# A two-block kernel on one core: unit matrix and scaled receptances of the WKV step matrices added by VectorE on eviction

## What is computed

```python
def step(s, inp):
    r_t, lw_t, k_t, v_t, a_t, b_t = inp
    sa = jnp.einsum('dbhij,dbhj->dbhi', s, a_t)
    s = s * jnp.exp(lw_t)[..., None, :] + sa[..., None] * b_t[..., None, :] + v_t[..., None] * k_t[..., None, :]
    return s, jnp.einsum('dbhij,dbhj->dbhi', s, r_t)

def rwkv_run(prep, s0):
    r, logw, k_dir, v, a_vec, b, gate = prep
    return wkv_scan(orient_shared(r), orient_dir(logw), orient_dir(k_dir), orient_shared(v),
                    orient_shared(a_vec), orient_dir(b), s0)
...
bonus = jnp.sum(r[None] * k_dir * r_k, axis=(0, -1))[..., None] * v
o = (yn + bonus.reshape(B, T, D)) * jax.nn.silu(gate)
```

## Time and profile before

| | |
|---|---|
| runs | 2570.5, 2577.51, 2576.24 us; median 2576.24 |
| profiled execution | 2568.52 us |
| its span | 2566.8 us |
| granted TensorE clock, mean | 0.937 |
| TensorE busy | 2276.0 us (89%), 16920 records |
| DVE busy | 974.0 us (38%) |
| ACT busy | 522.6 us (20%) |
| POOL busy | 319.0 us (12%) |

### The profile page before, as it was taken

The page is one execution under the profiler, slowest core; times in us unless marked ns, Lnnn a source line. Parts: engine busy times, 40 slices in busy tenths (PEclk is TensorE's granted clock), DMA queues, the critical chain, the costliest instruction groups (busy, mean ns, idle before and its releaser), DMA issues. The chain is left out here.

```text
span 2566.8 us, 40218 instructions
## 1 busy us (share of the span) xinstructions
PE 2276.0 (89%) x16920; PEld 1682.1 (66%) x16920; DVE 974.0 (38%) x2194; ACT 522.6 (20%) x926; POOL 319.0 (12%) x558
## 2 busy tenths in 40 slices
PE   2999966789999999999998688999998899879998
PEld 1888855578788886688873345565566667446546
DVE  3124436430343057277316244424424531120253
ACT  1011012320100010200013334333333422011142
POOL 0000000000000030000003544333432011000000
PEclk9999987799999999999999789998999889889989
DMA  7455520414686421187504665545544241313100
GB/s 298 184 225 218 197 100 0 81 23 161 273 303 232 177 104 50 66 332 297 207 1 163 215 171 161 148 124 139 137 122 110 49 112 44 150 51 117 47 1 17
DMA packets 126267, 359.75 MB, mean 140 GB/s; under 512 B 78600, under 2 KB 87048, under 8 KB 108304
## 3 DMA queue, kind: packets, MB, share of 16 engines
q1 hardware_dynamic: 93776, 213.05, 24.2%
q0 software_dynamic: 31744, 143.16, 16.5%
q10 hardware_dynamic: 576, 1.05, 0.1%
HBM read 340.36 MB, written 16.85 MB: 139 GB/s over the span
## 5 line engine op out<-in xcount | busy, mean ns | idle before, releaser
L271 PE MATMUL bank<-h,ring 128*128 128x256 f32 x2944 | 638.2, 380 | 4.8 <-DVEq L975 3.3
L271 PEld LDWEIGHTS bank<-h,ring 128*128 128x128 f32 x2944 | 560.3, 190 | 84.7 <-DVEq L975 4.9
L1755 PE MATMUL bank<-rw_feed 128*128 128x512 f32 x464 | 255.4, 658 | 22.3 <-DMA rw_feed<-in_rkvg 22.2
L185 PE MATMUL bank<-con 128*128 128x512 f32 x290 | 142.7, 644 | 91.9 <-PEq L257 57.6
L1571 POOL DMA_DIRECT2D rw_feed<-rwkv_mixes x232 | 124.5, 537 | 501.2 <-PE bank L1755 492.0
L185 PEld LDWEIGHTS bank<-con 128*128 128x128 f32 x290 | 58.0, 204 | 160.9 <-issue 160.3
L885 PE MATMUL bank<-ffn_hidden,ring 128*128 128x256 f32 x704 | 152.4, 379 | 3.4 <-PEq L911 3.4
L2056 DVE TENSOR_TENSOR rw_u<-bank,rw_lam 128x128 f32<-128x128 f32 x120 | 35.0, 291 | 301.8 <-PE bank L1702 298.3
L885 PEld LDWEIGHTS bank<-ffn_hidden,ring 128*128 128x128 f32 x704 | 133.6, 190 | 22.2 <-issue 4.1
L1755 PEld LDWEIGHTS bank<-rw_feed 128*128 128x128 f32 x464 | 79.3, 200 | 88.4 <-issue 45.7
L1572 POOL DMA_DIRECT2D rw_feed<-in_rkvg x232 | 124.2, 535 | 10.1 <-issue 10.1
(11 more groups left out here) (394 smaller groups left out, 3304.2 us busy)
## 6 DMA issues: line engine op xcount, KB each, us to landing
ring<-in_stream SPq DMA_DIRECT2D x81, 2048.0 KB, 8.1
rw_feed<-rwkv_mixes POOLq DMA_DIRECT2D x232, 256.0 KB, 3.0
next_w<-in_mod_stream POOLq DMA_DIRECT2D x24, 2048.0 KB, 10.4
ctx<-in_mod_rest POOLq DMA_DIRECT2D x16, 1024.0 KB, 7.2
rw_feed<-in_rkvg POOLq DMA_DIRECT2D x232, 64.0 KB, 3.2
rwkv_mixes<-mixed SPq DMA_DIRECT2D x8, 1024.0 KB, 3.9
y<-bias_table SPq DMA_DIRECT2D x48, 128.0 KB, 4.8
rw_at<-rw_at_kept SPq DMA_DIRECT2D x16, 256.0 KB, 5.7
```

The lines of the kernel that those rows point to most:

```text
L185: pe.matmul(k.psum[bank][:], const(k, "ident"), k.con[:, 0:512], start=True, stop=True)
L271: mm = pe.matmul(out, ring_tile(k, n, kt, i * P), rhs[kt], start=start and kt == kts[0], stop=stop and kt == kts[-1])
L1755: pe.matmul(k.psum[PROJ], feed[:, g % FEED, 512:], feed[:, g % FEED, 0:512], start=(kt == 0), stop=(kt == KT - 1)).then_inc(eaten, 1)
```

## The change

DVE takes over the eviction of the `gr` items from ACT, and adds the unit matrix and the receptances there, with two sums per bank. The 8 products with `ident` are gone, and the KP products begin their own groups (`start=True`). The unit matrix for all 128 partitions is built once, in the first block of the stage, in the free half of the constant `tri`. The list of items, the banks and the projections stay as they are.

```diff
@@ -1428,6 +1428,7 @@
         ysq = ysb
         U, lam = sb("u", 2, 2, 64), sb("lam", 4, 2, NCK)
         starts, gmask, sel, half2 = k.par[:, 0:512], const(k, "tri")[:, 0:64], sb("sel", 512), sb("half2", 6)
+        unit = const(k, "tri")[:, 64:P]
         cen, omka, eps = const(k, "neg"), sb("omka", KT), sb("eps", 1)
         kst, kstT, rst, rstT = sb("kst", 8), const(k, "flip"), sb("rst", 8), sb("rstT", P)
         feed = sb("feed", FEED, 512 + P)
@@ -1507,6 +1508,7 @@
                 nc.vector.memset(er.rearrange("p (c s) -> p c s", s=LCH)[:, :, LCH - 1], 1.0)
                 nc.vector.memset(en.rearrange("p (c s) -> p c s", s=LCH)[:, :, LCH - 1], 1.0)
                 nc.vector.memset(eps, GN_EPS)
+                nc.vector.tensor_tensor(unit, ident[:, 0:64], ident[:, 64:P], ALU.add)
                 kas = row(k, "rw", 0, 9 * KT).rearrange("p (n j) -> p n j", j=9)[:, :, KA]
                 nc.vector.tensor_scalar(omka, kas, -1.0, 1.0, ALU.mult, ALU.add)
                 nc.vector.scalar_tensor_tensor(cen, headones, -1.0 / 64, ident, ALU.mult, ALU.add)
@@ -1667,22 +1669,12 @@
                 pe.wait_ge(pq_down, 4 * u + 2 * half + 2)
                 pe.wait_ge(btok_down, 2 * u + 2)
                 outs = [take("gr", n, d, half, h) for h in range(2)]
-                for h in range(2):
-                    for e in range(2):
-                        unit = ident[rows64(e), rows64(e)]
-                        to = outs[h][rows64(e), 0:384].rearrange("p (c v) -> p c v", c=4)
-                        rt = RT[n % 2][d][rows64(e), 256 * half:256 * half + 256].rearrange("p (c h t) -> p c h t", h=2,
-                                                                                           t=LCH)
-                        pe.matmul(to[:, :, 0:64], unit, unit.unsqueeze(1).to_broadcast([64, 4, 64]), start=True, stop=False,
-                                  skip_group_check=True)
-                        pe.matmul(to[:, :, 64:96], unit, rt[:, :, h, :], start=False, stop=False, skip_group_check=True)
                 for j in range(4):
                     for h in range(2):
                         c2 = 4 * half + j
                         for e in range(2):
                             mm = pe.matmul(outs[h][rows64(e), 96 * j:96 * j + 96], KP[d][brows(h), c2, e, :],
-                                           BG[n % 3][d][brows(h), c2, e, 0:96], start=False, stop=True,
-                                           skip_group_check=True)
+                                           BG[n % 3][d][brows(h), c2, e, 0:96], start=True, stop=True)
                 mm.then_inc(gr_up, 1)
                 for h in range(2):
                     free(gr_down, 4 * u + 2 * half + h + 1, "gr", n, d, half, h)
@@ -1921,15 +1913,6 @@
                     x, y = VQ[n % 2][d][:, 4 * half, e, 0:1], KP[d][:, 4 * half, e, 0:1]
                     dst = bass.AP(y.tensor, y.offset, [list(y.ap[0]), [P, 4], [x.offset - y.offset, 2], [1, 64]])
                     nc.scalar.copy(dst, bank(*item).rearrange("p (c b v) -> p c b v", c=4, b=2)).then_inc(pq_down, 1)
-                elif kind == "gr":
-                    d, half = item[2:]
-                    act.wait_ge(gr_up, 2 * (2 * n + d) + half + 1)
-                    if n >= 2:
-                        act.wait_ge(step_up, (NCK + 1) * (n - 1))
-                    for h in range(2):
-                        dst = GR[n % 2][d].rearrange("p (c h) v -> p c h v", h=2)[:, 4 * half:4 * half + 4, h, :]
-                        nc.scalar.copy(dst, bank(*item, h)[:, 0:384].rearrange("p (c v) -> p c v", c=4)).then_inc(
-                            gr_down, 1)
                 elif kind == "read" and item[2] == 1:
                     act.wait_ge(yc_up, n + 1)
                     if n:
@@ -2047,6 +2030,17 @@
                         dve.wait_ge(o_out, 16 * (n - 3))
                     v.tensor_tensor(o[:, n % 4, :], bank("bonus", n, 0), vb(n), ALU.mult).then_inc(
                         bon_down, 1)
+                elif kind == "gr":
+                    d, half = item[2:]
+                    dve.wait_ge(gr_up, 2 * (2 * n + d) + half + 1)
+                    if n >= 2:
+                        dve.wait_ge(step_up, (NCK + 1) * (n - 1))
+                    rt = RT[n % 2][d][:, 256 * half:256 * half + 256].rearrange("p (c h t) -> p c h t", h=2, t=LCH)
+                    for h in range(2):
+                        dst = GR[n % 2][d].rearrange("p (c h) v -> p c h v", h=2)[:, 4 * half:4 * half + 4, h, :]
+                        src = bank(*item, h)[:, 0:384].rearrange("p (c v) -> p c v", c=4)
+                        v.tensor_tensor(dst[:, :, 0:64], src[:, :, 0:64], unit.unsqueeze(1).to_broadcast([P, 4, 64]), ALU.add)
+                        v.tensor_tensor(dst[:, :, 64:96], src[:, :, 64:96], rt[:, :, h, :], ALU.add).then_inc(gr_down, 1)
                 elif kind == "inv":
                     solve(n, item[2])
                 elif kind == "chain" and item[2] < NCK - 1:
```

## The result

The changed kernel runs at 2595.8 us (median of 4 runs, 2593.0 to 2597.4) against 2576.4 us before (4 runs, 2570.5 to 2577.5). The ratio is 1.0079, 95% interval 1.0061 to 1.0096: 0.8% slower. The forecast was 2575 us, no change to be measured, with a range up to 2586.

What follows compares the result with a forecast made beforehand. TensorE was taken to bound the scan, with DVE waits returning 30 of 48 us: -18.4 plus 17 for the clock gives -1.4, 2567 us profiled, 2575 as median; range 2555 to 2586.

Steps and rivals of the forecast that it cites:

- Products removed: Unit products at the head of each of 32 step-matrix calls: 1.50 us each, 48 us of TensorE at full clock.
- DVE's sums: Four new sums per call on DVE, one operand in PSUM: 1.1 us back to back, 1.4 as the bound.
- First calls: Direction 0: TensorE waits 2.8 us for bonus input; loses 1.3 in four rounds, nothing for n=2 to 4.
- Second calls: Direction 0: next turn waits for DVE's bonus bank; -0.4 us n=0 to 4, +0.5 n=5 and 6, -1.5 n=7.
- Third and fourth calls: Direction 1, inversion steps: -3.0 us n=1 to 4 and 7, -2.5 n=0; DVE bounds n=5 and 6, -1.4 and -0.6.
- Rounds n = 2 to 4: Scan rounds of tiles 2 to 4, first to fourth calls together: each 3.4 us shorter.
- slower rival: Low clock outlasts 1798 in n=2 to 4, lasts 20 us after n=5 and 6: +9.5, 2586 us; chance 0.17.
- Direction 1: The third and fourth calls' half of the change, by the sum without the clock: -19.5 us.
- The clock: New 2.8 us pauses behind first calls start low-clock stretches in four more rounds, costing 17 us.
- the term of 17 us: Price of new low-clock stretches: 5 us for n=0 and 1 plus 12 for n=5 and 6; bounds 0 and 24.
- the 12 us for n = 5 and 6: Low-clock price behind their first calls: 6.0 us each, from 13 us stretches losing 0.46 of their time.
- the 13 us: Length of low clock expected behind first calls of n=5 and 6, read from the stretch after 2027.34 up to 2040.3.

Runs made afterwards that it cites:

- direction 1 alone: The change made only for the third and fourth calls, the other calls as in the kernel before: 2556.4 us, ratio 0.9937 to before.
- the pause away in two rounds: The changed kernel with DVE taking the bonus item first only behind the calls of n = 5 and 6: 2566.1 us, ratio 0.9974 to before.
- the bonus first: The changed kernel with DVE taking each bonus item ahead of the step-matrix item it follows in the list: 2536.7 us, ratio 0.9869 to before.
- direction 0 alone: The change made only for the first and second calls, the other calls as in the kernel before: 2583.7 us, ratio 1.0052 to before.

## Why the prediction was wrong, step by step

- **Products removed, 1.50 us a call, 48 us.** Right: 47.7 us when they alone were left out.
- **DVE's sums, 1.1 us a call.** Right: from 1970.30 to the next item's start at 1971.37, 1.07 us; the pieces 0.42 and 0.28.
- **First calls, a pause of 2.8 us in seven rounds.** Right in place and number, 2.65 us.
- **Second calls.** At n=5 the turn waits 1.96 us for the bonus bank, as laid out; the call's own length there was at the low clock.
- **Third and fourth calls.** Right in place: behind the fourth call of n=5 DVE works without a gap from the sums (2012.24) to the chain's multiply, and TensorE waits for it. How much that took of the two late rounds wasn't measured apart.

```profile
2015.21 0.29 DVE L2050 TENSOR_TENSOR rw_u<-bank,rw_lam 128x128 f32<-128x128 f32 x1
2015.65 0.35 PE L1694 MATMUL bank<-rw_u,rw_gr 64*64 64x64 f32 x5 [0.29 <-DVE rw_u L2050]
```

- **Rounds n = 2 to 4, 3.4 us shorter each.** Right: 3.5, 3.4 and 3.2. The low stretches of these rounds stayed at 10 us, so that part of the slower rival did not happen.
- **Direction 1, -19.5 us.** Right: -18.2 when done alone.
- **The clock.** This is the step that failed, the term of 17 us, and in it the 12 us for n = 5 and 6. That low stretches would start there was right. By the Trainium skill's rule on pauses ("TensorE: Matmul & The Clock Gate", "Why this matters for your kernels"), which warns of idle gaps above some 3 us, pauses of 2.65 us should leave the clock up. The trace doesn't agree: at n=5 such a pause ends at 1972.89, and the clock is low from 1974. The size was wrong: 13 us of low clock were put behind each of the two first calls, with 20 as the bound. Measured, n=5's round has 32 us more of it than before and n=6's 59: 27 and 41 us in the new stretches behind the first calls, and 20 us more in the one at the end of n=5's round, which runs on into n=6's. From n=5's first call on low time grew by 91 us (61 to 152). The two rounds are 36 us longer, where 0.4 and 1.2 were laid out without the clock: 35 us instead of 12. For n = 0 and 1 together 3 and 14 us of new low clock stand in the trace; the two rounds are 0.2 and 2.6 us longer where -1.6 and -2.1 were laid out, so 6.5 us stand against the 5 put there.
- **Where the 13 us came from.** They were counted from 2027.34, where TensorE resumes, to 2040.3. In the same trace the clock was already low before, and a stretch of 23 us, with TensorE busy in 22.14 of them, follows at the end of n=6's round:

```profile
2020.00:2027.00 7.00, 1.43 (x20) 0.91 (x18) 6.58 (x19) 2.08 (x5) 0.00 (x0) 0.50 0.25 37
2092.00:2115.00 23.00, 22.14 (x222) 15.41 (x224) 5.83 (x24) 5.56 (x9) 1.38 (x3) 0.50 0.55 175
```

  So the kernel before had stretches of 20 and 24 us in these rounds, and neither 13 us nor the bound of 20 was safe by its own trace.
- **The sum with the measured low time.** 107 us more of it in the scan x 0.46 = 49; -18.4 + 49 = +31. The end of the scan came 22.5 us later (2199.2 to 2221.8) and the span grew by 26.9. The sum is 8 us too high: the clock cost 22.5 + 18.4 = 41 us, 0.38 of the low time and not 0.46. That part of it fell where TensorE would have waited for DVE anyway is likely and not shown.

The slower rival named this mechanism and gave 2586; it bounded a stretch by 20 us where 41 were measured. The error in method was to take the length of a stretch as a property of the pause, from one row. The pause only starts it: a stretch that follows no bonus pause was 20, 24, 34 or 41 us long at the same place, the end of n=5's round, in the kernel before, with direction 1 alone, with the pause away in two rounds, and with the bonus first. What sets the length stays open.

## What to carry to other kernels

When work moves to another engine, look first at what stands behind it in that engine's order, and put what TensorE waits for ahead of it: here that exchange of neighbouring items turns 0.8% slower into 1.3% faster. A short pause in a stretch of small products should be priced with the low clock behind it, up to 41 us here, and not with its own length. Read the clock over the whole stage before pricing it, as the longest stretches of the kernel before were the warning here. Where such a pause can't be removed, product work whose result is overwritten can pay: 16 products, two ahead of each bonus product, were worth 31 us. Twelve in the calls were worth 10 us with the pauses away and nothing with them.

## What was not expected of the hardware

- A useless product can make the kernel faster: two of 128x512 in each bonus item, 2595.8 to 2564.4 us.
- The clock stayed low for 41 us while TensorE was 91% busy (37.34 of 41 us from 2069 to 2110 of the changed kernel, granted 0.51). With the bonus first it was low while TensorE was busy in 24.89 of 25 us, in the row of 2000 to 2025 above.

```profile
2069.00:2110.00 41.00, 37.34 (x430) 26.50 (x431) 11.51 (x43) 5.97 (x9) 3.36 (x7) 0.51 0.15 38
```

- The low-clock time isn't the same in each execution: with direction 0 alone ten runs had mean granted clocks from 0.920 to 0.932 and took 2576 to 2602 us, the shortest at the highest clock, while four of the changed kernel had 0.913 to 0.915 and took 2593 to 2597. One profiled execution shows one such draw.
- What exactly lets the clock rise again stays open. Twelve full-size products shortened the low time by 54 us without the pauses and by 35 with them.
